# Expert products in plain float32 on four column groups, with a ring of 14 weight blocks

## The chip, the cores and the metric

The kernel runs on one core of a Trainium2 chip. The metric is the device time of one launch in microseconds (us). TensorE multiplies, reading from the on-chip memory and writing into eight banks of accumulators; VectorE, ScalarE and GpSimd work elementwise; SyncE here only issues transfers. The engines run on their own and meet at semaphores.

## The reference

One inference step of a trunk of two layers for 256 prompt tokens and 8 x 4 sample tokens (288 in all, width 1024), in float32. Layer 0 has gated linear attention and a dense SwiGLU, layer 1 an mLSTM and a mixture of 8 experts, two for each token. The change touches the mixture alone:

```
probs = softmax(x @ w_router + b_router)
top_p, top_i = top_k(probs, 2);  top_p = top_p / sum(top_p)
gates = sum(one_hot(top_i, 8) * top_p[..., None], axis=-2)
for e in range(8):
    g, u = split(x @ w_gu[e], 2)          # w_gu[e]: 1024 x 7168
    y = y + gates[:, e:e+1] * ((silu(g) * u) @ w_down[e])   # w_down[e]: 3584 x 1024
```

An expert's weights are 44.0 MB of float32, all eight 352 MB, read once.

## The kernel before

Everything ahead of the mixture (both mixers, the dense block, router, table of tokens) runs first. Then comes a loop over items, one item for an expert with up to 96 of its tokens (`CAP`); with these inputs it makes 8 passes. In one pass:

- **Weights.** The 44 MB come as 42 blocks (`PER`) of 1 MB into a ring of 7 (`RING`), each 128 partitions x 2048 floats (`SLOT`). A gate or up block has four row tiles of 512 columns (rows of 2 KB in memory), a down block two row tiles of 1024 columns (rows of 4 KB). SyncE issues a load when `wlo_ready` says that VectorE has finished with the block seven back (line 739).
- **Split.** TensorE multiplies here in the faster format float32r, which keeps fewer bits. So every block is split: `weight_hi` on ScalarE (line 2142) writes the rounded part into `w_hi`, `weight_lo` on VectorE (line 2874) the rest into `w_lo`, each with three places (`SPLIT`). The tokens (`xg_hi`, `xg_lo`) and the activations (`aT_hi`, `aT_lo`) are split as well, and `three` (lines 1090 to 1092) makes each product of hi x hi, hi x lo and lo x hi, with 96 stationary columns of tokens and 512 moving columns of weights. Some of these tiles lie in memory called `hT_split` or `hT`; the profile shows those names.
- **Steps.** The 3584 hidden columns are taken in 7 steps (`STEPS`) of 512. `project("g", n)` and `project("u", n)` fill gate and up banks, two of each (`GB`, `UB`) in turn. ScalarE takes Silu of the gate bank (line 2182), VectorE multiplies with the up bank (line 2934), `turn_act` transposes the result on TensorE (line 1724) one step later, and `down` adds its product into the banks `YB`, behind the up product of the next step.
- **End of a pass.** `next_tokens` transposes the next expert's tokens (line 1753). `item_rows` (line 1673) turns the next item's gates and rows. In the next pass ScalarE scales the finished output into `ye` (`read_output`), GpSimd adds it into rows in memory (a scatter with addition) and gathers the tokens for the pass after.

The last item's output stays on the chip: `read_output` and `output_lo` split it, and `scatter` (lines 1688 and 1689) spreads it over the tokens with matmuls, before the final norm.

Each engine runs its instructions in the order in which they are written. `loop_full(b, k, i)` waits until bank b is filled for the k-th time in pass i, `loop_before(b, k, i)` until it is free for that.

Of the kernel before, what the change touches and what calls it, by code (L numbers as in the profile page):

```python
# [24 lines left out]
P = 128  # L25
# [7 lines left out]
TT = 3  # L33
# [16 lines left out]
RING = 7  # L50
EARLY_RING = 4
LATE_ORDER = (6, 4, 5, 2, 3, 0, 1)
SPLIT = 3
# [9 lines left out]
WIDE = 512  # L63
STEPS = FE // WIDE
HALF = KT // 2
PER = 6 * STEPS
# [140 lines left out]
GB, UB, YB, TB, MB = (0, 1), (2, 3), (4, 5), 6, 7  # L207
LAST = ((GB[0], 0), (GB[1], 0), (UB[0], 0), (UB[1], 0), (TB, 0), (MB, 1))
GAB = (GB[1], UB[1])
GATE_ROW = 32  # L210
LOW_ROW = 32
LOOP_TURNS = {0: 4, 1: 4, 2: 4, 3: 4, 4: 1, 5: 1, 6: STEPS, 7: 1}
# [4 lines left out]
def trunk_kernel(nc, ins, outs):  # L217
# [5 lines left out]
    with ExitStack() as ctx:  # L223
# [6 lines left out]

        with nc.sbuf_tensor("ring", [P, RING * SLOT], F32) as ring:
            pass
        ring_lo = sb("ring_lo", [P, RING * SLOT], F32R)
# [43 lines left out]
        rank_rows = sb("rank_rows", [RANK, 10, T])  # L277
# [123 lines left out]
        w_hi = es("w_hi", [P, SPLIT, SLOT], F32R)  # L401
        w_lo = es("w_lo", [P, SPLIT, SLOT], F32R)
        xg_hi = es("xg_hi", [P, KT, CAP], F32R)
        xg_lo = es("xg_lo", [P, KT, CAP], F32R)
        aT_hi = [es("aT_hi", [P, 4, CAP], F32R)[:, :, :]]
        aT_lo = [es("aT_lo", [P, 4, CAP], F32R)[:, :, :]]
        for n, a in enumerate((aT_hi, aT_lo)):
            at = 3 * WIDE + n * 4 * CAP
            a.append(hT_split[:, at:at + 4 * CAP].rearrange("p (f c) -> p f c", f=4))
        h_tok = es("h_tok", [P, TT, D])  # L410
        x_acc = es("x_acc", [P, TT, D])
        hT_flat = hT[0:CAP, :, :].rearrange("p k t -> p (k t)")
        sg = hT_flat[:, 0:2 * WIDE].rearrange("p (a n) -> p a n", a=2)
        act = hT_flat[:, 2 * WIDE:3 * WIDE]
# [31 lines left out]
        whi_ready = sem("whi_ready")  # L446
        wlo_ready = sem("wlo_ready")
        hi_ready = sem("hi_ready")
        split_used = sem("split_used")
# [114 lines left out]
        def expert_slot(j):  # L564

            s = LATE_ORDER[j % RING]
            return ring[:, s * SLOT:(s + 1) * SLOT], s
# [48 lines left out]
        late_free = [full("L1r5"), full("L1r7"), full("L1r7"), full("L1w1"), full("L1w3"), full("L1w5"), full("L1w7")]  # L616
# [33 lines left out]
        expert_order = [(k, 0, x) for k in "gu" for x in range(2)]  # L650
        for j in range(1, STEPS):
            expert_order += [(k, j - (k == "d"), x) for k in "gud" for x in range(2)]
        expert_order += [("d", STEPS - 1, x) for x in range(2)]
        assert len(expert_order) == PER
        expert_at = {x: n for n, x in enumerate(expert_order)}

# [4 lines left out]
        def split_free(eng, j, i):  # L661

            if j == SPLIT - 1:
                eng.wait_ge(bank_full[YB[1]], i + static_turns[YB[1]])
                return
            if j < SPLIT:
                used_ = i * SPLIT_COUNT + (split_counts[PER - SPLIT + j] - SPLIT_COUNT + 2)
            else:
                kind, nth, x = expert_order[j - SPLIT]
                if kind != "d" and x == 1:  # L670
                    eng.wait_ge(*loop_full((GB if kind == "g" else UB)[nth % 2], nth // 2, i))
                    return
                used_ = i * SPLIT_COUNT + (split_counts[j - SPLIT] + 2)
            eng.wait_ge(split_used, used_)


        token_after = {2: (0,), 3: (1, 2), 4: (3,), 5: (4,), 6: (5,), 7: (6, 7)}

        split_counts, SPLIT_COUNT = {}, 0
        for j, (kind, nth, x) in enumerate(expert_order):  # L680
            if (kind != "d" and x == 0) or (kind == "d" and j < PER - 1):
                SPLIT_COUNT += 1
                split_counts[j] = SPLIT_COUNT
        HI_TURNS = STEPS + 2

        def turned_hi(ac, nth, i):

            ac.wait_ge(*loop_full(TB, nth, i))
            ac.activation(aT_hi[nth % 2], psum[TB][:, 0:4 * CAP].rearrange("p (f c) -> p f c", f=4), ACT.Copy).then_inc(hi_ready, 1)
# [5 lines left out]
        def _(sp):  # L695
# [33 lines left out]
            def load(e, j):  # L729
                kind, nth, x = expert_order[j]  # L730
                dst, s = expert_slot(j)
                if kind == "d":
                    r = nth * WIDE + x * 2 * P
                    src = w_dn[bass.ds(e, 1), r:r + 2 * P, :].rearrange("e (t p) n -> p (e t) n", p=P)
                else:
                    c = nth * WIDE + (FE if kind == "u" else 0)
                    src = w_gu[bass.ds(e, 1), x * HALF * P:(x + 1) * HALF * P, c:c + WIDE].rearrange("e (t p) n -> p (e t) n", p=P)
                out = dst.rearrange("p (k n) -> p k n", k=src.shape[1])
                sp.dma_start(out, src).then_inc(slot_loaded[s], 16)

            for j in range(PER):
                if j < RING:
                    sp.wait_ge(*late_free[j])
                else:
                    sp.wait_ge(wlo_ready, j - RING + 1)
                load(0, j)
# [287 lines left out]
        def _(pe):  # L1034
# [664 lines left out]
            with pe.Fori(0, n_items) as i:  # L1699
# [27 lines left out]
                def down(nth, xs=(0, 1)):  # L1727
                    pe.wait_ge(*loop_before(TB, nth + 1, i))
                    if nth == 0:
                        output_read(i)  # L1730
# [1278 lines left out]
```

## Time and profile before

| | |
|---|---|
| median of 3 runs | 1524.95 us (1524.89 to 1526.27) |
| profiled execution, its span | 1524.6 us |
| TensorE busy | 1508.8 us, 99% |
| VectorE, ScalarE, GpSimd busy | 1219.2, 1009.9, 186.9 us |
| moved by transfers | 449.97 MB, mean 295 GB/s |
| matmul records | 8481 |

The loop over experts takes the span from 547.9 us to about 1510; some 14 us follow. The times of matmuls in the profile overlap, since they are pipelined: what a matmul costs is read from how far apart two starts are. A plain float32 matmul has two records, a float32r matmul one. In a form such as 128\*96, 128x512 the first pair is the stationary operand (rows by columns), the second the moving one. The rows below are not repeated here.

### The profile page before, as it was taken

To read this page: it belongs to the slowest core of one execution; us is meant where nothing else is said; L and a number is where in the kernel's file an instruction comes from. 1 tells how busy PE (TensorE), PEld (TensorE's weight loads), DVE (VectorE), ACT (ScalarE), POOL (GpSimd) and SP (SyncE) were. 2 spreads that over 40 slices of the span, in tenths; PEclk is the share of its full clock that TensorE was granted. 3 is DMA by queue.
4 is the path that set the end of the run, shared out by engine and by line. 5 is a ranking of instruction groups with operands and counts; after the bars stand their busy time and mean duration, and the time that the engine had idled before them with its cause. 6 is when DMAs were issued, how large, how long until landed. Compare 5 with 4: busy or idle time off the path is not lost.

```text
span 1524.6 us, 22920 instructions
## 1 busy us (share of the span) xinstructions
PE 1508.8 (99%) x8481; PEld 1196.9 (79%) x8481; DVE 1219.2 (80%) x1189; ACT 1009.9 (66%) x871; POOL 186.9 (12%) x224
## 2 busy tenths in 40 slices
PE   9999999999999999999999999999999999999997
PEld 7999999999998977777776776776776777767775
DVE  6758766646776688888889888888888888888888
ACT  5646533335546487787787777778778778778776
POOL 3334100002234150000000000000000000000010
PEclk9999999999999999999999999999999999999999
DMA  7467555455453689999999999999999999999993
GB/s 215 140 198 234 163 166 166 159 180 181 141 136 112 219 298 388 383 350 394 375 348 394 371 364 380 370 366 376 377 379 361 376 382 358 377 383 355 387 372 131
DMA packets 234264, 449.97 MB, mean 295 GB/s; under 512 B 16713, under 2 KB 83345, under 8 KB 234209
## 3 DMA queue, kind: packets, MB, share of 16 engines
q1 hardware_dynamic: 226208, 422.98, 77.5%
q0 software_dynamic: 7376, 24.53, 5.6%
q10 hardware_dynamic: 624, 1.70, 0.3%
q8 instruction: 37, 0.61, 0.2%
q14 instruction: 19, 0.15, 0.0%
HBM read 434.62 MB, written 14.57 MB: 295 GB/s over the span
## 4 chain that ended last, share of the span: by engine, by line
PE 96%; DVE 2%; ACT 1%; issue 1%; DMA 0%; SPq 0%; DVEq 0%; ACTq 0%
PE bank L1090 29%; PE bank L1092 29%; PE bank L1091 29%; PE bank L1724 1%; PE bank L1328 1%; PE bank L1058 0%; PE bank L1317 0%; PE bank L1658 0%; PE bank L1638 0%; PE bank L1296 0%; PE bank L1753 0%; DMA par_rows<-in_mlstm_g_norm_dram 0%; PE bank L1554 0%; PE bank L1308 0%; PE bank L1239 0%
## 5 line engine op out<-in xcount | busy, mean ns | idle before, releaser
L2874 DVE TENSOR_TENSOR w_lo<-ring,w_hi 128x2048 fp32r<-128x2048 f32 x337 | 771.4, 2291 | 121.6 <-ACT w_hi L2142 120.1
L2142 ACT ACTIVATE w_hi<-ring 128x2048 fp32r<-128x2048 f32 x337 | 645.4, 1918 | 223.5 <-PE bank L1092 223.4
L1090 PE MATMUL bank<-w_hi,xg_hi 128*96 128x512 f32 x896 | 355.9, 397 | 1.0 <-DVE xg_lo L2884 1.0
L1092 PE MATMUL bank<-w_hi,xg_lo 128*96 128x512 f32 x896 | 353.4, 394 | 0.0
L1091 PE MATMUL bank<-w_lo,xg_hi 128*96 128x512 f32 x896 | 351.8, 393 | 0.0
L1092 PE MATMUL bank<-work_split,ring_lo 128*128 128x288 f32 x920 | 271.4, 295 | 0.0
L1090 PE MATMUL bank<-work_split 128*128 128x288 f32 x904 | 268.8, 297 | 0.5 <-DVE ring_lo L2319 0.4
L1091 PE MATMUL bank<-work_split 128*128 128x288 f32 x904 | 266.0, 294 | 0.0
L1092 PEld LDWEIGHTS bank<-w_hi,xg_lo 128*96 128x96 f32 x896 | 144.6, 161 | 63.1
L1090 PEld LDWEIGHTS bank<-w_hi,xg_hi 128*96 128x96 f32 x896 | 144.5, 161 | 61.3 <-DVE w_lo L2874 2.1
L1091 PEld LDWEIGHTS bank<-w_lo,xg_hi 128*96 128x96 f32 x896 | 144.9, 162 | 59.7
L1092 PEld LDWEIGHTS bank<-work_split,ring_lo 128*128 128x128 f32 x920 | 172.8, 188 | 0.0
L1090 PEld LDWEIGHTS bank<-work_split 128*128 128x128 f32 x904 | 169.9, 188 | 3.5 <-issue 1.6
L1091 PEld LDWEIGHTS bank<-work_split 128*128 128x128 f32 x904 | 170.0, 188 | 0.2
L1847 ACT ACTIVATE work_split<-ring 128x2048 fp32r<-128x2048 f32 (+1 forms) x49 | 91.8, 1875 | 85.8 <-PE bank L1092 76.7
L2506 DVE TENSOR_TENSOR ring_lo<-ring,work_split 128x2048 fp32r<-128x2048 f32 (+1 forms) x34 | 75.6, 2224 | 34.3 <-ACT work_split L1847 34.2
L1092 PE MATMUL bank<-w_hi,aT_lo 128*96 128x512 f32 x256 | 101.1, 395 | 0.0
L1090 PE MATMUL bank<-w_hi,aT_hi 128*96 128x512 f32 x256 | 100.7, 393 | 0.0
L1091 PE MATMUL bank<-w_lo,aT_hi 128*96 128x512 f32 x256 | 100.4, 392 | 0.0
L1024 POOL TENSOR_TENSOR turn_mark<-pad_row 1x1 f32<-1x1 f32 x8 | 17.8, 2231 | 509.6 <-DVE row_next L2897 509.6
L1090 PE MATMUL bank<-w_hi,hT_split 128*96 128x512 f32 x192 | 76.6, 399 | 0.0
L1091 PE MATMUL bank<-w_lo,hT_split 128*96 128x512 f32 x192 | 75.8, 395 | 0.0
(456 smaller groups left out, 1686.4 us busy)
## 6 DMA issues: line engine op xcount, KB each, us to landing
ring<-in_moe_w_gu_dram SPq DMA_DIRECT2D x225, 1024.0 KB, 6.3
ring<-in_moe_w_down_dram SPq DMA_DIRECT2D x112, 1024.0 KB, 6.2
ring<-in_ffn_w_gu_dram SPq DMA_DIRECT2D x22, 1024.0 KB, 5.1
ring<-in_gla_w_in_dram SPq DMA_DIRECT2D x12, 1024.0 KB, 5.4
ring<-in_mlstm_w_in_dram SPq DMA_DIRECT2D x12, 1024.0 KB, 5.3
ring<-in_ffn_w_down_dram SPq DMA_DIRECT2D x8, 1024.0 KB, 5.0
out_dram<-work POOLq DMA_DIRECT2D x9, 512.0 KB, 4.5
work<-in_state_gla_S_dram POOLq DMA_DIRECT2D x8, 512.0 KB, 7.5
```

The source lines that it names most:

```text
L1024: gp.tensor_tensor(turn_mark[:, :], pad_row[0:1, :], pad_row[0:1, :], ALU.add).then_inc(marked, 1)
L1090: pe.matmul(out, w_hi_, x_hi, start=first, stop=False, skip_group_check=True)
L1091: pe.matmul(out, w_hi_, x_lo, start=False, stop=False, skip_group_check=True)
L1092: return pe.matmul(out, w_lo_, x_hi, start=False, stop=last, skip_group_check=True)
L1328: mm = pe.matmul(bk[:, m * n:(m + 1) * n], v_tok[0:n, tt, g * P:(g + 1) * P], scores(g), start=(m == 0), stop=done, skip_group_check=True)
L1724: mm = pe.transpose(psum[TB][:, f * CAP:(f + 1) * CAP], act[:, f * P:(f + 1) * P], ident[0:CAP, 0:CAP])
L1847: ac.activation(hi, raw, ACT.Copy).then_inc(fhi_ready, 1)
L2142: ac.activation(w_hi[:, j % SPLIT, :], src, ACT.Copy).then_inc(whi_ready, 1)
L2506: ve.tensor_tensor(lo, raw, hi.bitcast(F32), ALU.subtract).then_inc(flo_ready, 1)
L2874: ve.tensor_tensor(w_lo[:, j % SPLIT, :], src, w_hi[:, j % SPLIT, :].bitcast(F32), ALU.subtract)\
```

## The change

The expert products are made in plain float32, without `w_hi`, `w_lo`, `weight_hi`, `weight_lo` and the split of tokens and activations. The 96 tokens are three tiles of 32 (`TILE`, `TILES`). A matmul now has 32 stationary columns, 256 moving columns, and one of four column groups of the array: its output goes to 32 of the 128 partitions of a bank. Three token tiles and four groups don't fit each other, so the fourth group takes another part of the product: in a step's first two column halves (`gate, 0` and `gate, 1`), bank AB holds three tiles of half 0 and one of half 1, BB the same of up, CB the four that are left. For the output, columns 768 to 1023 are spread over the fourth groups of the other three quarters.

```
-RING = 7
+RING_MEM = 7
-LATE_ORDER = (6, 4, 5, 2, 3, 0, 1)
+LATE_ORDER = (6, 4, 5, 2, 7, 3, 0, 12, 13, 1, 8, 9, 10, 11)
+RING = len(LATE_ORDER)
+WIDTHS = (512,) * 7
-GB, UB, YB, TB, MB = (0, 1), (2, 3), (4, 5), 6, 7
+AB, BB, CB, YB, TB, MB = 0, 1, 2, (4, 5), (6, 3), 7
...
+                def gate_up(s, xs):
+                    n = WIDTHS[s] // 2
+                    per = SLOT // (4 * n)
+                    for x in xs:
+                        w = weights("gu", s, x)
+                        for k in range(per):
+                            kt = x * per + k
+                            gate, up = (w[:, (4 * k + o) * n:(4 * k + o + 2) * n].rearrange("p (c n) -> p c n", c=2) for o in (0, 2))
+                            x_tile = [xg[:, kt, a * TILE:(a + 1) * TILE] for a in range(TILES)]
+                            for b, units in ((AB, ((gate, 0, 0), (gate, 0, 1), (gate, 0, 2), (gate, 1, 0))),
+                                             (BB, ((up, 0, 0), (up, 0, 1), (up, 0, 2), (up, 1, 0))),
+                                             (CB, ((up, 1, 1), (up, 1, 2), (gate, 1, 1), (gate, 1, 2)))):
+                                if first:
+                                    pe.wait_ge(*loop_before(b, s, i))
+                                for group, (m, c, a) in enumerate(units):
+                                    mm = part(psum[b][:, 0:n], group, x_tile[a], m[:, c, :], first, last)
+                                    if b == AB and group == 0 and k == 0:
+                                        mm.then_inc(slot_begun, 1)
...
+                            for d, b in enumerate((YB[0], YB[0], YB[1])):
+                                for group, (m, a) in enumerate(((d, 0), (d, 1), (d, 2), (3, d))):
+                                    mm = part(out, group, act_tile(s, x, t, a), w[:, t, m, :], first and d != 1, last)
...
+                gate_up(0, range(2 * blocks(0)))
+                for s in range(1, STEPS):
+                    gate_up(s, range(2))
+                    turn_act(s - 1)
...
+                    gate_up(s, range(2, 2 * blocks(s)))
+                    if s < STEPS - 1:
+                        down(s - 1, range(blocks(s - 1)))
+                s = STEPS - 1
+                down(s - 1, range(2))
+                next_tokens(i)
+                turn_act(s)
+                down(s - 1, range(2, blocks(s - 1)))
+                down(s, range(blocks(s)))
```

- **Banks.** Gate, up and the mixed bank exist once each (before, two of gate and two of up). The transposed activations take two banks (`TB`), one copied by VectorE (128x256), one by ScalarE (128x128). A step has four transposes, two of 128 and two of 64 moving columns.
- **ScalarE and VectorE** per step: Silu of AB (128x256) and of half of CB (64x256), and the two multiplications `act1` and `act2`.
- **Ring.** 14 blocks instead of 7, the new seven in the memory of `w_hi` and `w_lo`. A load may start once TensorE has begun the block after the one that lay there (`slot_begun`), without the other engines. A gate/up block holds two row tiles of 512 gate and 512 up columns, loaded by two transfers of 512 KB; a down block has two neighbouring rows for each partition, rows of 8 KB:

```
-                    src = w_dn[bass.ds(e, 1), r:r + 2 * P, :].rearrange("e (t p) n -> p (e t) n", p=P)
+                    src = w_dn[bass.ds(e, 1), r:r + 2 * P, :].rearrange("e (p t) n -> p (e t) n", t=2)
```

- **Output.** `last_quarter` on VectorE gathers columns 768 to 1023 from the fourth groups (three copies, then a scaling), ahead of the steps of each pass and once behind the loop, where it stands ahead of `output_lo`.

```
+            last_quarter(n_items)
             output_lo(0)
             ve.wait_ge(*loop_full(MB, 0, n_items))
...
             output_lo(1)
+            output_lo(2)
```

ScalarE, head of a pass, before: Silu of the first gate bank (bank 0), with the table load ahead of it; between them stand copies of blocks into `w_hi`.

```order
L2156 ACTIVATE xT<-bank,slot_gate 96x512 [waits bank_free5,bank_full5]
L2139 REGISTER_ALU
L674 REGISTER_ALU [waits slot_loaded2]
L2142 ACTIVATE w_hi<-ring 128x2048 [waits split_used]
L671 ISA [waits slot_loaded3]
L2142 ACTIVATE w_hi<-ring 128x2048 [waits bank_full0]
L2181 REGISTER_ALU [waits bank_full0]
L2182 ACT_TABLE_LOAD
L2182 ACTIVATE hT<-bank,one_col 96x512 [waits bank_free2]
```

And now, with bank 0 for AB, bank 1 for BB and bank 2 for CB:

```order
L2167 ACTIVATE xT<-bank,slot_gate 96x256 [waits bank_free5,bank_full5]
L2184 ISA
L2185 REGISTER_ALU [waits bank_full0]
L2186 ACT_TABLE_LOAD
L2186 ACTIVATE hT<-bank,one_col 128x256 [waits bank_free1]
L2187 ISA
L2188 REGISTER_ALU [waits bank_full2]
L2189 ACTIVATE hT<-bank,one_col 64x256 [waits bank_free2]
```

The copies are gone; the table load still stands behind the wait for bank 0 and ahead of Silu.

TensorE, end of a pass, before: the last transposes of activations (line 1724) stand between two halves of the down product of step 5 (12 matmuls each).

```order
L1092 MATMUL bank<-w_hi,hT_split 96x512
L1724 MATMUL bank<-ident,hT 128x96 [waits bank_free6,bank_free2]
L1724 MATMUL bank<-ident,hT 128x96 x3
L1703 REGISTER_ALU [waits bank_free6]
L1090 MATMUL bank<-w_hi,hT_split 96x512 [waits wlo_ready]
L1091 MATMUL bank<-w_lo,hT_split 96x512
```

And now (banks 6 and 3 hold the transposed activations; `rank_rows` is the memory of tokens and activations):

```order
L1693 MATMUL bank<-ring,rank_rows 32x256 x23
L1769 ISA
L1772 REGISTER_ALU [waits gathered]
L1775 MATMUL bank<-ident,xT 128x96 [waits bank_free0]
L1775 MATMUL bank<-ident,xT 128x96 x3
L1775 MATMUL bank<-ident,xT 128x96 [waits bank_free1]
L1775 MATMUL bank<-ident,xT 128x96 x3
L1728 MATMUL bank<-ident,hT 128x128 [waits bank_free6,bank_free3,bank_free2,bank_free1]
L1728 MATMUL bank<-ident,hT 128x128
L1733 MATMUL bank<-ident,hT 128x64 x2
L1750 REGISTER_ALU [waits bank_free6,bank_free3]
L1688 REGISTER_ALU [waits bank_free3]
```

The whole down product of step 5 stands ahead of the transposes, and that of step 6, which reads what they make, right behind them.

## Rows read from the trace of the kernel before

**Rows 1.** The page: busy time by engine, and the chain that ended last.

```profile
PE 1508.8 (99%) x8481; PEld 1196.9 (79%) x8481; DVE 1219.2 (80%) x1189; ACT 1009.9 (66%) x871; POOL 186.9 (12%) x224
PE 96%; DVE 2%; ACT 1%; issue 1%; DMA 0%; SPq 0%; DVEq 0%; ACTq 0%
```

**Rows 2.** The loop: length, busy us by engine, clock, share and GB/s of transfers.

```profile
668.00:1500.00 832.00, 832.00 (x3777) 585.08 (x3776) 725.54 (x456) 631.65 (x428) 43.44 (x32) 1.00 1.02 372
```

**Rows 3.** TensorE in one pass by form: count, busy us and mean ns, idle.

```profile
L1091 PE MATMUL bank<-w_lo,xg_hi 128*96 128x512 f32 x112 | 44.0, 393 | 0.0
```

**Rows 4.** Timeline of TensorE around `next_tokens`, two passes: start, us, instruction.

```profile
655.66 0.39 PE L1091 MATMUL bank<-w_lo,xg_hi 128*96 128x512 f32 x1
655.89 0.39 PE L1092 MATMUL bank<-w_hi,xg_lo 128*96 128x512 f32 x1
656.12 0.82 PE L1753 MATMUL bank<-ident,xT 96*128 96x96 f32 x8
...
776.42 0.82 PE L1753 MATMUL bank<-ident,xT 96*128 96x96 f32 x8
```

**Rows 5.** Line 1368 and its neighbours: durations (min/median/max ns), timeline, one stretch as above.

```profile
L1368 PE MATMUL bank<-work x64: 379/379/403, 103.7 to 107.0; 128*32 128x256 f32 x64
...
102.80 0.94 PE L1328 MATMUL bank<-work 32*128 32x32 f32 x7
103.67 3.66 PE L1368 MATMUL bank<-work 128*32 128x256 f32 x64
107.26 0.98 PE L1308 MATMUL bank<-work_split 128*128 128x256 f32 x6
...
104.00:104.40 0.40, 0.40 (x16) 0.23 (x12) 1.00 1.04 420
```

**Rows 6.** Timeline of TensorE at its densest stretch.

```profile
465.63 1.97 PE L1328 MATMUL bank<-work 32*128 32x32 f32 x16
467.52 0.63 PE L1554 MATMUL bank<-work,head_col 32*8 32x32 f32 x16
468.08 0.63 PE L1589 MATMUL bank<-work,head_col 128*8 128x32 f32 x16
...
468.86 3.71 PE L1604 MATMUL bank<-work 128*64 128x128 f32 x64
```

**Rows 7.** ScalarE and VectorE by form; the last two are of the whole kernel.

```profile
L2182 ACT ACT_TABLE_LOAD x1 | 1.3, 1283 | 0.0
...
L2874 DVE TENSOR_TENSOR w_lo<-ring,w_hi 128x2048 fp32r<-128x2048 f32 x43 | 98.4, 2290 | 15.7 <-ACT w_hi L2142 15.5
...
L2922 DVE TENSOR_TENSOR aT_lo<-bank,aT_hi 128x384 fp32r<-128x384 f32 x4 | 2.2, 552 | 0.0
...
L1898 ACT ACTIVATE work<-bank 128x256 f32<-128x256 f32 x16 | 5.2, 379 | 19.3 <-PE bank L1152 19.3
...
L2296 DVE TENSOR_TENSOR work<-bank,rbc 128x256 f32<-128x256 f32 x16 | 6.7, 420 | 9.1 <-PE bank L1092 9.0
```

**Rows 8.** Waits of SyncE's queue from 560 to 1500: us in total, times, longest.

```profile
SPq L739 <- DVE w_lo L2874: 734.5, 325, 3.6
```

**Rows 9.** Transfers: first pass's q8, queues of 668 to 1500 (first, last), a small one, 580 to 600.

```profile
q8 instruction: 5, 0.08, 0.3%
...
q1 hardware_dynamic: 127236, 302.51, 98.5%
...
q14 instruction: 3, 0.02, 0.0%
...
out_dram<-par_rows POOLq DMA_DIRECT2D x1, 16.0 KB, 2.0
...
580.00:600.00 20.00, 20.00 (x97) 14.21 (x96) 17.22 (x10) 14.55 (x10) 0.00 (x0) 1.00 1.05 393
```

**Rows 10.** Timeline behind the loop: `ye_lo` on VectorE, the first scattering matmul.

```profile
1509.97 0.75 DVE L2234 SCALAR_TENSOR_TENSOR ye_lo<-bank,slot_gate,ye_hi 96x512 fp32r<-96x512 f32 x1
...
1511.65 0.49 PE L1688 MATMUL bank<-ye_hi,selT 96*128 96x512 f32 x1 [0.72 <-DVE selT L2961]
```

More of the change, by code:

```diff
@@ L62 @@
 N_STATIC = 2 * N_MIX + N_FFN
-WIDE = 512
-STEPS = FE // WIDE
+WIDTHS = (512,) * 7
+STEPS = len(WIDTHS)
+STARTS = [sum(WIDTHS[:s]) for s in range(STEPS)]
 HALF = KT // 2
-PER = 6 * STEPS
+TILE = 32
+TILES = CAP // TILE
+QUARTERS = D // 4
 WORK = 24576
@@ L648, in out_parts, with blocks @@
             return raw, out_hi[l][n], ring_lo[:, s * SLOT:(s + 1) * SLOT]
[L650 to L654, printed above, removed]
-        expert_at = {x: n for n, x in enumerate(expert_order)}
+        def blocks(s):
+            return WIDTHS[s] // (2 * P)
@@ new lines, in part @@
+                def part(out, group, stationary, moving, first, last):
+                    return pe.matmul(out[group * TILE:(group + 1) * TILE, :], stationary, moving, start=first, stop=last, skip_group_check=True)
+                def gate_up(s, xs):
[3 more added lines that the diff above has]
+                        w = weights("gu", s, x)
+                        for k in range(per):
+                            kt = x * per + k
+                            gate, up = (w[:, (4 * k + o) * n:(4 * k + o + 2) * n].rearrange("p (c n) -> p c n", c=2) for o in (0, 2))
+                            x_tile = [xg[:, kt, a * TILE:(a + 1) * TILE] for a in range(TILES)]
+                            first, last = kt == 0, kt == KT - 1
+                            for b, units in ((AB, ((gate, 0, 0), (gate, 0, 1), (gate, 0, 2), (gate, 1, 0))),
[7 more added lines that the diff above has]
+                                        mm.then_inc(slot_begun, 1)
+                                if last:
+                                    mm.then_inc(bank_full[b], 1)
@@ new lines, in act_tile, with down @@
+                def act_tile(s, x, t, a):
+                    n = WIDTHS[s] // 2
+                    c, y = divmod(x, n // (2 * P))
+                    q = 2 * y + t
+                    if c == 0 or a == 0:
+                        at = q * P + (a if c == 0 else TILES) * TILE
+                        return aT[s % 2][0][:, at:at + TILE]
+                    at = q * 64 + (a - 1) * TILE
+                    return aT[s % 2][1][:, at:at + TILE]
+                def down(s, xs):
+                    for b in TB:
+                        pe.wait_ge(*loop_before(b, s + 1, i))
+                    if s == 0 and xs[0] == 0:
@@ L2962, in _ @@
             output_lo(1)
+            output_lo(2)
             ve.wait_ge(x_back, 48)
```

353 lines of the change are left out of this document (157 added, 196 removed).

## The prediction

> **What bounds the kernel now.** I read the page first: TensorE is busy 99% of the span and the chain that ended last is 96% TensorE [rows 1]. Then the stretches: in the 832 us from 668 to 1500, all of it the loop over experts, TensorE is never idle and its clock is fully granted (1.00, the 2.4 GHz level), VectorE and ScalarE are busy 87% and 76%, and the transfers run at 372 GB/s with a share of 1.02 [rows 2]. So the loop is bound by TensorE, with the transfers close behind. How long is one expert? The eight transposes of the next tokens come once per expert, at 656.12 and at 776.42 [rows 4]: 120.3 us, eight times, 962.4 us of the span.
>
> What is in these 120.3 us? 42 blocks of 12 matmuls, 504 in all (28 blocks of gate and up give 336, of which 112 for each of three lines, [rows 3]), and the spacing of neighbours is 0.23 us (655.66, 655.89, 656.12 in [rows 4]; their 0.39 us of duration overlap). 504 x 0.232 = 117 us; 28 transposes, 8 of next tokens at 0.082 us ((0.82 - 0.25)/7) and 6 records of `item_rows` are the other 3.4 us. A split matmul of 512 columns is thus spaced by 0.232 us, though 512 columns at 2.4 GHz are 0.213.
>
> **The change, part by part.**
>
> *The products.* Float32 shows as two records per matmul, each of two cycles per column. The kernel before has this very shape once: line 1368 multiplies with 32 stationary columns, 256 moving columns, four column groups, 32 matmuls, 64 records [rows 5]. They start at 103.67 and the next line at 107.26, 3.59 us for 16 rounds of four records; without the two changes of tiling (below) 16 x 0.216 = 3.46. So four matmuls run at once and a round of four costs 2 x 0.216 = 0.432 us, and this while transfers ran at 420 GB/s (the stretch from 104.0 in [rows 5]). The changed loop needs per step 8 row tiles x 3 rounds for gate and up and 4 x 3 for down: 36 rounds, 252 per expert. 252 x 0.432 = **108.9 us**, against 117. The array does as many column cycles as before; the gain is the spacing of 216 against 232 ns.
>
> *Transposes.* Per step two with 128 moving columns (0.11 us, as line 1328 in [rows 5]: (0.94 - 0.27)/6) and two with 64, between nothing and 0.11; I take 0.07, a little under the 0.082 of 96 columns. 14 x 0.11 + 14 x 0.07 + 8 x 0.082 + 0.5 = **3.7 us**.
>
> *Changes of tiling.* Into line 1368: previous start plus 0.112 would be 103.58, it is 103.67: 0.09. Out: 0.13 (above). 0.22 us for there and back, six times per expert (the seventh lies in a stall, below): **1.3 us**. Bounds: nothing, and double.
>
> *New wait 1.* Gate, up and their mixed bank are now single (AB, BB, CB), and after step 0 no down product stands between two gate/up groups. ScalarE's order in the changed kernel has a table load behind the wait on bank 0: the load of 1.28 us [rows 7] starts only when AB is full. AB is full some 0.2 us after its last round, then 1.28 + about 0.45 for Silu on 256 columns (the 0.38 of a copy [rows 7] plus its bias), then 0.2 to TensorE: 2.25 us, of which rounds of BB and CB cover 0.86. **1.4 us** per expert. Behind it queue VectorE's two multiplications (0.42 each [rows 7]), which arrive just in time for BB and CB. In later steps the down product (5.2 us) covers the same chain.
>
> *New wait 2.* At the end of an expert, `turn_act(6)` is followed at once by `down(6)`, where before half a down product (2.8 us) stood between. VectorE first copies half of the new tokens (128x384, 0.55 [rows 7]), then the transposed activations (about 0.42): some 1.25 us after the transposes began, plus 0.2, against 0.35 of work: **1.1 us**.
>
> *Code.* The loop's body grows from 543 matmuls to 1047. In the first pass five pieces of code were fetched, in the next 832 us q8, the queue that carries code, has no line (q1 first, q14 last), so the body stayed at hand [rows 9]. Whether a body of twice the size does, no row shows. If not, each return to the loop's head waits for a fetch. A piece has 16 KB, and the nearest transfer of 16 KB took 2.0 us from issue to landing [rows 9]. Bounds: nothing, and 4 us for a loaded queue; I take 1.2 us for each of 7 returns, since matmuls already queued cover a part: **8 us**. The Trainium skill ("Runtime: NRT & Kernel Launch", Instruction fetch mechanics) gives TensorE room for 2048 instructions, refilled in blocks, and says that a taken branch to code outside the window stalls; by it this body (two instructions per matmul, 2094) would just not fit. The trace agrees only as far as that the smaller body fitted.
>
> *What goes.* 42 copies of whole blocks on ScalarE and 42 subtractions of 2.29 us on VectorE per expert [rows 7]. Both lay beside TensorE, so they give back nothing; they only stop being next in line.
>
> *Transfers.* 44.0 MB of weights per expert as before plus 0.8 of rows. The ring of 14 blocks lets some 12 be loaded before 548 us. SyncE waited for free blocks 734.5 us of the loop [rows 8], so 372 GB/s was what was asked for; from 580 to 600 it was 393 [rows 9]. Down rows of 8 KB instead of 4 should cost no more. 346 MB must land in 940 us: 368 GB/s. **Nothing**, as long as that is given.
>
> *Ends.* Behind the loop VectorE now moves the last quarter (three copies and a scaling, some 0.4 us each) before `output_lo(0)`, which scattering waits for; before, `ye_lo` began at 1509.97 and scattering at 1511.65 [rows 10]. With the third `output_lo`: **+2 us**. Ahead of the loop one subtraction goes: -0.4.
>
> *Sum.* 108.9 + 3.7 + 1.3 + 1.4 + 1.1 = 116.4 us; x 8 = 931.2; + 8.4 of code = 939.6, against 962.4. 1524.6 - 962.4 + 939.6 + 1.6 = 1503.4. The median of the runs is 0.35 above the span, so **1504 us**.
>
> **Rivals.**
>
> *TensorE's dispatch is the bound (slower).* The loop asks for a record pair (weights and matmul) every 54 ns for 110 us on end; before it was every 232. Line 1368 asked it only for 3.5 us, out of a filled queue. For: the densest stretch has 16 + 16 + 64 records (and one of a transpose) from 467.52 to 472.57 [rows 6], 52 ns each, and is no longer than 5 us. Against: it held without a gap, and records 29 ns apart just before it ((0.63 - 0.19) / 15, lines 1554 and 1589) left little queued for the 64. It decides above 54 ns. If the rate were that of the stretch from 465.63, 113 records in 6.9 us or 61 ns, an expert took 2016 x 0.061 + 7.5 = 130.5 us, the kernel 1524.6 + 8 x 10.2 + 10 = some 1615. The Trainium skill ("TensorE: Matmul & The Clock Gate", Back-to-back issue gap) has about 62 ns per matmul of sequencer time as a possible bound; by it the time would be the same, some 1620. The 52 ns of this trace speak against it.
>
> *Transfers are the bound.* 12 or 13 blocks in flight may give less than two did. At 360 GB/s the 346 MB take 961 us, the last lands at 1509, and with 3 us for its products and 16 behind the loop the kernel takes 1528; it is slower than before under 361, and binds at all under 368. For: the share of 1.02 says that the engines always had a packet. Against: 393 above, and SyncE's waits.
>
> *All covers hold.* No code fetch, no cost of retiling, half the stalls: 114 us per expert, 1476.
>
> *The groups don't run at once.* Then an expert would take over 400 us. Line 1368 excludes it.
>
> **How the numbers follow.** TensorE bound with the terms above, 1485 to 1520: 0.62. All covers hold, 1474 to 1485: 0.08. Transfers bound: 0.12, half of it under 1522, the rest 1522 to 1535. Fetches or stalls larger than taken, up to 1540: 0.06. Dispatch bound, 1560 to 1650: 0.10. Groups not at once, or an order I misread: 0.02. The range from 1478 to 1532 leaves out dispatch, the last case and the edges. A measurement tells about 0.2%, 3 us, from no change: faster 0.80, same 0.06, slower 0.14.
>
> **What would show it.** Right: rounds of four records every 216 ns; an expert every 116 to 118 us; gaps of TensorE at two places only, behind step 0 (ended by ScalarE, with a table load in it) and before the last down product (ended by VectorE); q8 lines in the loop if code is fetched again. Wrong: gaps put down to issue all over the rounds, spaced over 54 ns per record (dispatch); TensorE waiting for blocks of the ring (transfers); rounds longer than 0.432 us without any gap (then the row of line 1368 did not carry over to a long stretch). In either of the last two the sum fails in its first term.

## The result, and the profile after

The changed kernel takes 1582.9 us (median of 4 runs, 1579.6 to 1584.5) against 1525.6 us of the kernel before (4 runs beside it): ratio 1.037, interval 1.036 to 1.039. It is slower by 3.7%, where 1.4% faster was forecast, and the time lies 51 us above the range. The profiled execution has a span of 1582.7 us.

The page of the changed kernel: busy time, chain, products and the queue that carries code. The first and the third line answer to [rows 1].

```profile
PE 1507.8 (95%) x20577; PEld 1085.0 (69%) x20577; DVE 474.1 (30%) x935; ACT 377.9 (24%) x583; POOL 153.2 (10%) x224
...
q8 instruction: 182, 2.98, 0.8%
...
PE 90%; issue 4%; DVE 4%; ACT 1%; DMA 0%; SPq 0%; DVEq 0%; ACTq 0%
...
L1693 PE MATMUL bank<-ring,rank_rows 128*32 128x256 f32 x16128 | 908.2, 385 | 59.0 <-issue 44.8
```

VectorE and ScalarE are relieved as meant (80% and 66% to 30% and 24%), TensorE is still the chain, but it is busy 95% in place of 99%, and 4% of the chain is "issue": time in which nothing that the profile shows was waited for. The loop in windows (columns as in [rows 2]): all of it, a stretch without a return to the loop's head, and one with.

```profile
668.00:1500.00 832.00, 777.58 (x13262) 454.36 (x13266) 77.00 (x222) 80.86 (x166) 21.10 (x32) 0.96 0.96 349
...
1200.00:1300.00 100.00, 100.00 (x1762) 59.77 (x1755) 9.42 (x28) 7.57 (x19) 1.12 (x2) 1.00 1.01 376
1300.00:1400.00 100.00, 89.90 (x1537) 52.46 (x1539) 9.47 (x28) 10.21 (x20) 2.75 (x4) 0.95 0.94 338
```

Where nothing returns, TensorE is full, at full clock, and executes 1762 records in 100 us. Where the loop returns, 10 us are idle and the clock is lower. The timeline of TensorE there (start, us, instruction, count, in brackets the idle time before and what ended it), and the windows of the same place:

```profile
664.24 2.13 PE L1693 MATMUL bank<-ring,rank_rows 128*32 128x256 f32 x36
670.79 0.83 PE L1693 MATMUL bank<-ring,rank_rows 128*32 128x256 f32 x9 [4.43 <-issue]
674.14 8.13 PE L1693 MATMUL bank<-ring,rank_rows 128*32 128x256 f32 x108 [2.51 <-issue]
...
664.50:672.50 8.00, 2.70 (x45) 1.17 (x37) 1.63 (x4) 1.04 (x2) 1.65 (x2) 0.94 0.82 252
...
672.50:682.00 9.50, 7.86 (x108) 4.07 (x112) 0.00 (x0) 0.00 (x0) 0.00 (x0) 0.69 0.66 199
```

Two stalls, 4.43 and 2.51 us, with nine records between them, and then a clock of 0.69: most of the stretch from 672.5 to 682 ran at the 1.2 GHz level (in windows of 2 us the clock is 1.00 until 670, then 0.90, then 0.50 from 672 to 678, 0.89, and 1.00 from 680). The expert's products themselves are not slow. The waits of TensorE from 560 to 1560 (total, times, longest) show the same twice per return, 14 times in seven returns:

```profile
PE bank L1693 <- issue: 44.8, 14, 4.8
...
PE bank L1693 <- ACT hT L2186: 7.6, 7, 1.1
PE bank L1693 <- ACT rank_rows L2174: 4.3, 7, 0.6
```

So the two stalls of a return are 6.4 us on average (44.8 / 7), the first 4.09 to 4.80, the second 1.18 to 3.60. The trace also holds a record of the branch itself, which the page leaves out. It lasts 5.2 to 5.9 us at each of the seven returns; in the kernel before it lasts 0.21 to 0.24.

And one trip of the loop, 1050.1 to 1178.7, in the transfers (packets, MB, share) and in the window:

```profile
q8 instruction: 19, 0.31, 1.0%
...
1050.10:1178.70 128.60, 121.05 (x2066) 70.64 (x2062) 11.98 (x34) 12.65 (x26) 2.76 (x4) 0.96 0.96 351
```

The body is fetched anew on every trip, 19 packets of 16 KB, where the kernel before had no line of q8 in its loop [rows 9]. A pass takes 128.5 us ((1558.3 - 787.3) / 6, from starts of `next_tokens`), against 120.3 before [rows 4] and 117.6 by my sum. The same window also corrects a count: 2066 matmul and 2062 weight load records lie in the window of a pass (some cross its edges; 2058 of each start in it), each an instruction. A float32 matmul is two pairs of weight load and matmul, not one; the body has 4,187 instructions, not the 2,094 of the prediction (all records of TensorE and its sequencer in a trip; before, 1,168).

### The profile page after: what moved, and what is told of

It reads as the page before. It is cut to its first block, busy times and chain, and to the rows that moved or that the text cites. A ratio compares the mean times of both kernels' runs of the same rounds, so it can differ in the third digit from the quotient of the medians.

```text
span 1582.7 us, 46658 instructions
## 1 busy us (share of the span) xinstructions
PE 1507.8 (95%) x20577; PEld 1085.0 (69%) x20577; DVE 474.1 (30%) x935; ACT 377.9 (24%) x583; POOL 153.2 (10%) x224
## 4 chain that ended last, share of the span: by engine, by line
PE 90%; issue 4%; DVE 4%; ACT 1%; DMA 0%; SPq 0%; DVEq 0%; ACTq 0%
PE bank L1693 57%; PE bank L1073 8%; PE bank L1075 8%; PE bank L1074 8%; PE bank L1728 1%; PE bank L1733 1%; PE bank L1309 1%; DVE ring_lo L2284 1%; PE bank L1775 0%; PE bank L1041 0%; PE bank L1298 0%; PE bank L1639 0%; PE bank L1619 0%; PE bank L1277 0%; DMA par_rows<-in_mlstm_g_norm_dram 0%
## 5 line engine op out<-in xcount | busy, mean ns | idle before, releaser
L1693 PE MATMUL bank<-ring,rank_rows 128*32 128x256 f32 x16128 | 908.2, 385 | 59.0 <-issue 44.8
L1693 PEld LDWEIGHTS bank<-ring,rank_rows 128*32 128x32 f32 x16128 | 519.2, 111 | 424.5 <-issue 77.8
L2935 DVE COPY rank_rows<-bank 128x256 f32<-128x256 f32 x56 | 23.7, 423 | 426.2 <-PE bank L1728 426.2
L2953 DVE TENSOR_TENSOR hT<-hT,bank 128x256 f32<-128x256 f32 x56 | 23.6, 421 | 378.6 <-ACT hT L2186 378.6
L2186 ACT ACTIVATE hT<-bank,one_col 128x256 f32<-128x256 f32 x56 | 26.5, 474 | 207.5 <-PE bank L1693 207.4
L1002 POOL TENSOR_TENSOR turn_mark<-pad_row 1x1 f32<-1x1 f32 x8 | 1.5, 183 | 702.3 <-DVE xT L2928 702.3
L1074 PE MATMUL bank<-hT_split,ring_lo 128*128 128x288 f32 x128 | 37.8, 295 | 0.0
L2284 DVE TENSOR_TENSOR ring_lo<-ring,work_split 128x2048 fp32r<-128x2048 f32 x15 | 34.6, 2307 | 7.6 <-ACT work_split L1867 7.5
L1073 PE MATMUL bank<-ring_lo 128*128 128x288 f32 x112 | 34.2, 305 | 0.1
L1075 PE MATMUL bank<-ring_lo 128*128 128x288 f32 x112 | 33.0, 295 | 0.0
L1728 PEld LDWEIGHTS bank<-ident,hT 128*128 128x128 f32 x112 | 17.5, 205 | 19.8 <-issue 19.8
```

The lines of the kernel that those rows point to most:

```text
L1073: pe.matmul(out, w_hi_, x_hi, start=first, stop=False, skip_group_check=True)
L1074: pe.matmul(out, w_hi_, x_lo, start=False, stop=False, skip_group_check=True)
L1075: return pe.matmul(out, w_lo_, x_hi, start=False, stop=last, skip_group_check=True)
L1693: return pe.matmul(out[group * TILE:(group + 1) * TILE, :], stationary, moving, start=first, stop=last, skip_group_check=True)
L1728: mm = pe.transpose(psum[TB[0]][:, q * P:(q + 1) * P], act1[:, 2 * P * y + t:2 * P * (y + 1):2], ident[:, :])
L2186: ac.activation(sg1[:, 0:n], psum[AB][:, 0:n], ACT.Silu, bias=zero).then_inc(bank_free[AB], 1)
```

## The experiments

All times are medians. The kernel before, run beside each group, took 1526.1 us (e1 to e4), 1525.0 (e5 to e8) and 1526.3 (e9 to e12), so a difference between runs of two groups is uncertain by about 1 us.

**e1: no return.** TensorE's pass is written out seven times, and its loop runs once.

```
-            with pe.Fori(0, n_items) as i:
+            def one_pass(i):
...
+            for n in range(7):
+                one_pass(n)
+            with pe.Fori(7, n_items) as i:
+                one_pass(i)
```

> The changed kernel with TensorE's expert pass written out seven times ahead of its loop, which then runs once: the same matmuls, waits and transfers, but no backward branch on TensorE's path. Theory (the missed time is instruction fetch at the seven returns of a loop of about 4,100 instructions): each pass loses the gaps of 4.8 and 2.9 us after the branch and the stretch at 1.2 GHz behind them, about 11 us in all, so 1583 - 7 x 11 = about 1505 us, granted clock 1.00 in every window of the expert stage, pass about 117.5 us. Rival A (matmuls are bound by dispatch, or the four column groups interfere): the pitch inside the passes does not change and the time stays within 5 us of 1583. Rival B (transfers take over once TensorE is not held up): the pass cannot be shorter than 44.04 MB at the rate of the undisturbed window 1200:1300 (376 GB/s), 117.1 us, so the same 1505 but with waits on the ring in the list of waits; if the rate sustained over all passes is only 349 GB/s, the pass is 126 us and the time about 1570.

Measured: 1515.9 us (ratio 0.9937, 0.992 to 0.9953), 67.0 us less than the changed kernel, 9.6 for each of seven returns. The loop's window and page lines of e1:

```profile
668.00:1450.00 782.00, 770.43 (x13550) 474.06 (x13546) 78.02 (x224) 82.20 (x169) 20.92 (x31) 1.00 1.03 380
...
L1693 PE MATMUL bank<-ring,rank_rows 128*32 128x256 f32 x16128 | 884.7, 379 | 14.3 <-ACT hT L2190 9.3
```

The clock is 1.00 throughout, "issue" is gone from the idle time, the transfers give 380 GB/s with SyncE waiting on TensorE for 434 of these 782 us, not the other way round. Dispatch is no bound: a record pair goes out every 54 ns on average, pass after pass. So the returns cost more than the kernel lost (67 us of 57), and the changed products are worth having. But the pass is 118.8 us ((1489.7 - 776.9) / 6), not 117.5, and the time 11 us above the theory's 1505. That rest is in other terms of the sum (e7, and the next section).

**e2: a hint ahead of the branch.**

```
-            with pe.Fori(0, n_items) as i:
+            with nc.Fori(0, n_items, engines=..., hint_back_edge=True) as i:
```

> The changed kernel, with one instruction more at the head of TensorE's loop: a hint that names the branch back, so that its target can be fetched ahead. Theory (code fetch at the returns): the hint takes away the first of the two gaps (4.8 us), perhaps the second (2.9 us) and with them the fall of the clock: 1583 - 7 x 5 = 1548 if only the first goes, 1505 if both go. Rival (the gap is not a fetch but the loop's register work, or some engine that is waited for): within 5 us of 1583.

Measured: 1566.4 us, 2.4 us less per return. Both stalls are still there; one return in the timeline of TensorE:

```profile
911.44 5.39 PE L1693 MATMUL bank<-ring,rank_rows 128*32 128x256 f32 x96 [0.61 <-ACT rank_rows L2174]
919.71 0.68 PE L1693 MATMUL bank<-ring,rank_rows 128*32 128x256 f32 x8 [2.88 <-issue]
922.59 1.93 PE L1693 MATMUL bank<-ring,rank_rows 128*32 128x256 f32 x16 [2.20 <-issue]
```

The hint names only code, and it moves the stall: this is about fetching. But it takes neither gap away, and my 1548 was too hopeful: together they go from 6.4 to 4.5 us on average (31.3 us in seven returns). The branch record falls from 5.2 to 5.9 us to 2.4 to 3.8. The last packet of q8 ahead of the branch's end starts 0.0 to 1.4 us behind the branch's start, without the hint 2.7 to 3.5, so that block is asked for earlier. The packet behind it still starts only after the branch's end, in every return of both kernels.

**e3: the kernel before with a body of two passes.** Nothing of the change is in this kernel.

```
-            with pe.Fori(0, n_items) as i:
-                (one pass)
+            with pe.Fori(0, n_items, 2) as i:
+                one_pass(i)
+                one_pass(i + 1)
```

> The kernel before, with two expert passes in each trip of TensorE's loop (four trips, three returns; some 2,280 instructions in the body where there were 1,140). Arithmetic, waits and transfers are those of before. Theory (a body that does not stay loaded is fetched again at each return and the chip stalls there): 3 returns x about 8 to 11 us = 1550 to 1559 us; the instruction queue shows some ten packets per return in the second half of the span, where before had none. Rival (the stalls of the changed kernel come from its column groups, its ring or its other order, not from the size of the loop): 1525.6 within 3 us.

Measured: 1542.7 us (1.0113, 1.0096 to 1.013), 5.5 us for each of three returns. One trip of it (q8, window), and its return in the timeline:

```profile
q8 instruction: 11, 0.18, 0.3%
...
1029.60:1275.50 245.90, 242.44 (x1094) 169.90 (x1093) 209.94 (x133) 183.09 (x125) 11.37 (x8) 0.99 1.01 366
...
1033.62 0.47 PE L1090 MATMUL bank<-w_hi,xg_hi 128*96 128x512 f32 x1 [0.51 <-issue]
...
1038.89 0.74 PE L1090 MATMUL bank<-w_hi,xg_hi 128*96 128x512 f32 x1 [2.96 <-issue]
1039.42 0.63 PE L1091 MATMUL bank<-w_lo,xg_hi 128*96 128x512 f32 x1
1039.85 0.63 PE L1092 MATMUL bank<-w_hi,xg_lo 128*96 128x512 f32 x1
```

(The window counts records, 1094 + 1093; with registers and branch a trip has 2,334 instructions.) The mechanism needs neither column groups nor the larger ring: a kernel whose loop was free of it gets it when its body doubles. The price was missed: 5.5 us, not 8 to 11. The second gap is not far from that in the changed kernel (2.96 and 2.51), the first is 0.51 in place of 4.43. Two things differ. The matmuls still queued at the branch are spaced by 0.23 us here and by 0.054 there, so here they cover more: they run 3.5 us past the start of the branch. And the branch record itself is shorter, 3.5 to 3.9 us for 5.2 to 5.9; why, the runs don't show. Behind the gap matmuls of 512 columns start 0.43 us apart (1039.42 and 1039.85), the 1.2 GHz level; ahead of it, 0.23.

**e4: wider steps, the loop kept.**

```
-WIDTHS = (512,) * 7
+WIDTHS = (1024, 1024, 1024, 512)
```

> The changed kernel with gate and up in steps of 1024, 1024, 1024 and 512 columns in place of seven of 512: 512-column matmuls for three quarters of the expert's input products, and 1,440 matmul records in a pass in place of 2,016, some 2,950 instructions; rows of 4 KB for the wide steps. Theory (code): the body is still too long to stay loaded, so the seven stalls stay: about 1583, less 0 to 8 us for the steps that are no longer there. Rival (each instruction costs dispatch time, or the price of a return goes with the length of the body): 720 fewer instruction pairs x 8 passes x some ns each, or stalls a third shorter: 1555 or less.

Measured: 1563.1 us (1553.6 to 1564.3), 20 less than the changed kernel, and outside both expectations. With e7, the same steps without a return, it comes apart: e4 - e7 is 72.6 us, 10.4 per return, no less than for the longer body (9.6). So the price does not go with the length of a body that is too long. The 20 us are not code: without any return the same steps save 25 (e7).

**e5: the table of Silu early.** On top of e1.

```
                 for b, ins_ in read_output(i, ye):
                     ins_.then_inc(bank_free[b], 1)
+                ac.activation(silu_seed[:, 0:1], one, ACT.Silu, bias=zero)
```

> The unrolled kernel (e1), with one Silu of a single column per partition put behind ScalarE's read of the outputs at the head of its pass, so that the table of Silu is loaded (1.28 us) before the first gate columns are complete, and not behind the wait for them. Theory (the stall of 1.55 us between step 0 and step 1 of every pass is this table load): the gap shrinks to some 0.3 us, 8 x 1.25 = 10 us less: about 1506 us. Rival (the stall is the Silu itself with the release of the bank, or the copies of VectorE): the gap stays above 1.2 us and the time at 1515 to 1516.

Measured: 1507.0 us, 8.9 less than e1. ScalarE in e1 (first two lines) and in e5 (last three):

```profile
794.01 1.28 ACT L2190 ACT_TABLE_LOAD   x1 [8.94 <-PE bank L1693]
795.30 0.47 ACT L2190 ACTIVATE hT<-bank,one_col 128x256 f32<-128x256 f32 x1
```

```profile
782.35 1.28 ACT L2184 ACT_TABLE_LOAD   x1
783.64 0.30 ACT L2184 ACTIVATE spare<-one_col 128x1 f32<-128x1 f32 x1
791.37 0.47 ACT L2191 ACTIVATE hT<-bank,one_col 128x256 f32<-128x256 f32 x1 [7.44 <-PE bank L1693]
```

The load now lies in idle time, and the stall behind step 0 (1.55 us between two starts) is 0.41. Wait 1 of the prediction was right in place, cause and size.

**e6: a down product behind the last turn.** On top of e1.

```
-                down(s - 1, range(2))
+                down(s - 1, range(1))
                 next_tokens(i)
                 turn_act(s)
-                down(s - 1, range(2, blocks(s - 1)))
+                down(s - 1, range(1, blocks(s - 1)))
```

> The unrolled kernel (e1), with the last block of down(5) moved behind the last turn of the activations, as the kernel before had it; 5.2 us of matmuls then stand between the turn of step 6 and down(6). Theory (the gap of 0.84 us at that place is the wait for the copies of the turned activations): it shrinks to the 0.21 us of the other such places, 8 x 0.63 = 5 us less: about 1511 us. Rival (another wait takes its place: the gather of the next tokens or the activations of step 6 are now asked for 2.6 us earlier): the same time, or up to 8 x 2 us more.

Measured: 1510.6 us, 5.3 less. TensorE at this place in e1 and in e6:

```profile
777.64 0.43 PE L1728 MATMUL bank<-ident,hT 128*128 128x128 f32 x2
778.00 0.45 PE L1733 MATMUL bank<-ident,hT 64*128 64x64 f32 x2
779.01 15.75 PE L1693 MATMUL bank<-ring,rank_rows 128*32 128x256 f32 x288 [0.56 <-ACT rank_rows L2178]
```

```profile
775.28 0.45 PE L1733 MATMUL bank<-ident,hT 64*128 64x64 f32 x2
775.66 5.60 PE L1693 MATMUL bank<-ring,rank_rows 128*32 128x256 f32 x100
```

Wait 2 is real, 0.66 us in a pass where I took 1.1.

**e7: wider steps without a return.** e1 with the edit of e4.

> The unrolled kernel (e1) with the steps of 1024, 1024, 1024 and 512 columns: four turns of the activations in a pass in place of seven. Theory (between two matmuls of the experts a turn takes about 1.1 us of TensorE, 0.9 more than the matmul round it follows, and that was undersized in my sum): three turns less in each of 8 passes, 2.8 us, make the pass 116.0 and the time about 1494. Rival (the transfers are at their limit: the windows of e1 show a share of 1.02 to 1.03 and 375 to 385 GB/s): 44.04 MB in 116.0 us are 380 GB/s; at 375 the pass is 117.4 and the time 1505, with waits on the ring.

Measured: 1490.5 us (0.9766, 0.9749 to 0.9782), 25.4 less than e1. The pass is 115.7 us ((1463.7 - 769.7) / 6), 3.1 less. The last turn of a pass and a wide one:

```profile
770.43 0.43 PE L1728 MATMUL bank<-ident,hT 128*128 128x128 f32 x2
...
771.16 31.17 PE L1693 MATMUL bank<-ring,rank_rows 128*32 128x256 f32 x384
...
808.19 0.74 PE L1728 MATMUL bank<-ident,hT 128*128 128x128 f32 x4
...
809.48 0.67 PE L1654 MATMUL bank<-gate_token,sel 128*96 128x2 f32 x6
```

The transposes are as many as before, 28 in a pass, but in four turns in place of seven. From its first transpose to the instruction behind it a wide turn takes 1.29 us (808.19 to 809.48), two narrow ones take 2 x 0.81 (e1), and the change of tiling ahead of it comes once in place of twice: some 1.5 of the 3.1 us. Wait 2 is gone as well (770.43 to 771.16 is 0.73, for 1.37 in e1), which is 0.6, and the stall behind step 0 is 0.6 shorter (0.57 of idle time for 1.17). The other 0.4 us lie in the 144 rounds of 512 columns: one starts every 0.429 us, for 2 x 0.216. So what wider steps give here is not the turns alone. The transfers follow:

```profile
668.00:1450.00 782.00, 778.13 (x9922) 344.58 (x9918) 69.84 (x166) 69.74 (x111) 21.12 (x32) 1.00 1.01 388
```

388 GB/s, where 375 was my rival's limit.

**e8 to e10: how long a body stays.** The kernel before, two passes per trip, with products left out to shorten the code. The helpers `two` and `one` are `three` without its last, and without its last two, matmuls.

```
-                            mm = three(psum[b][0:CAP, :], ...
+                            mm = (two if kind == "g" else three)(psum[b][0:CAP, :], ...
...
-                                mm = three(psum[YB[half]][0:CAP, :], ...
+                                mm = two(psum[YB[half]][0:CAP, :], ...
```

> The kernel before with two passes in each trip as in e3, but without the third of the three split products (the one with the low part of the activations) in the gate columns and in down: that part of the arithmetic is left out, and two passes have about 1,830 instructions in place of 2,280. Only the returns are looked at. Theory (what fits in the instruction memory is not fetched again, and the limit lies between the two): no fetches of the instruction queue after the first trip, and no gap over 0.5 us at the three returns; the Trainium skill (Runtime: NRT & Kernel Launch, Instruction fetch mechanics) puts TensorE's limit at 2,048. Rival (any body longer than that of before, 1,140, is fetched again): about seven packets per trip and gaps of 1 and 3 us at each return, as in e3.

> As e8, with the third of the three products left out everywhere: two passes of the kernel before in a trip, about 1,660 instructions (six and a half blocks of 256, where one packet of the instruction queue is one block). e8 was fetched again with 1,890 instructions, so a plain limit of 2,048 is out. Theory now (the fetcher runs on in sequence two blocks past the branch at the end of the loop, e8 took ten packets a trip for a body of eight, and these two push out the head): the body and two more blocks have to fit in eight; seven or eight blocks and two are nine or ten, so it is fetched again, about nine packets a trip, with the gaps of 5 and 3 us. Rival (the limit lies just under e8's size): no packets after the first trip.

> As e9, with the second product of the gate columns left out too: about 1,440 instructions in a trip, which lie in six or seven blocks of 256. Theory (body and two blocks ahead have to fit in eight): where the body touches six blocks nothing is fetched after the first trip and the returns cost nothing; where it touches seven it is fetched again. Rival (anything that is longer than the 1,170 instructions of before is fetched again): about eight packets a trip and gaps of 5 and 3 us at each return.

A trip of e8, then of e9 (q8 and window of each), and the windows of a trip of e10, in whose transfers q8 has no line, with its return:

```profile
q8 instruction: 9, 0.15, 0.3%
...
1001.40:1232.50 231.10, 204.46 (x869) 131.56 (x870) 207.47 (x133) 181.22 (x125) 11.88 (x8) 0.98 1.04 387
```

```profile
q8 instruction: 9, 0.15, 0.3%
...
1000.50:1231.30 230.80, 183.88 (x757) 112.25 (x757) 207.07 (x133) 180.54 (x125) 11.89 (x8) 0.98 1.04 388
```

```profile
1000.90:1230.80 229.90, 173.17 (x645) 105.90 (x645) 208.31 (x133) 181.10 (x125) 11.88 (x8) 0.89 1.04 390
...
1002.42 0.39 PE L1095 MATMUL bank<-w_hi,aT_lo 128*96 128x512 f32 x1
1002.91 1.18 PE L1090 MATMUL bank<-w_hi,xg_hi 128*96 128x512 f32 x4
```

With what is neither matmul nor weight load, the trips have 1,886, 1,662 and 1,438 instructions. The first two are fetched again, the third is not, and the stalls go with the fetch: e9 has six gaps put down to "issue", 20.4 us in all, e10 has none. The branch records say the same: 6.2 to 7.6 us in e8, 6.2 to 6.3 in e9, 0.22 to 0.25 in e10. My expectation for e8 was wrong: the Trainium skill ("Runtime: NRT & Kernel Launch", Instruction fetch mechanics) gives TensorE room for 2,048 instructions, and here 1,662 already do not stay; the measurement decides. The corrected theory was stated before e9 and e10, and both agree with it (e10 if its body touches six blocks and not seven): the fetcher runs one or two blocks past the end of the body, and what it brings in pushes out the head. A packet is a block of some 256 instructions (e1 takes 97 packets for six passes of 4,187, 259 each), and the trips of e3, e8, e9 and the changed kernel took 11, 9 to 10, 9 and 19 packets for bodies of 10, 8, 7 and 17 blocks. A plain limit somewhere between 1,438 and 1,662 fits as well; the two are not told apart. The return of e8 (TensorE, timeline):

```profile
1001.29 0.47 PE L1090 MATMUL bank<-w_hi,aT_hi 128*96 128x512 f32 x1 [0.96 <-DVE w_lo L2882]
...
1002.98 0.40 PE L1091 MATMUL bank<-w_hi,aT_lo 128*96 128x512 f32 x1
1008.03 0.74 PE L1090 MATMUL bank<-w_hi,xg_hi 128*96 128x512 f32 x1 [4.66 <-issue]
...
1013.56 0.59 PE L1090 MATMUL bank<-w_hi,xg_hi 128*96 128x512 f32 x1 [1.80 <-issue]
```

Here TensorE had waited for VectorE just before (the low parts of the weights), so that only eight matmuls, 2.1 us, were left when the branch began at 1001.40. The branch lasted 6.2 us, and the first gap is 4.66 us. The times of these three (1488.0, 1486.7 and 1483.4, one run each) say nothing of the returns: VectorE is at 90% and the transfers are at 387 to 390 GB/s with a share of 1.04, so that a part of each stall may have been covered by time that TensorE would have waited anyway.

**e11: the best version.** e7 with the edit of e5.

> e7 (unrolled, steps of 1024, 1024, 1024 and 512 columns) with the one-column Silu of e5. Theory: the gap of 1.16 us between step 0 and step 1 goes down to some 0.4 us, 8 x 0.75 = 6 us less: about 1484 to 1485. Rival (the transfers, 44.04 MB in a pass of 114.9 us or 383 GB/s, take over): the gain stays under 2 us and waits on the ring show.

Measured: 1485.5 us (0.9731, 0.9714 to 0.9747), 5.0 less than e7 and 40.7 less than the kernel before.

```profile
668.00:1450.00 782.00, 782.00 (x9998) 346.95 (x9994) 71.06 (x167) 70.60 (x117) 19.75 (x31) 1.00 1.00 387
```

TensorE has no idle time left, its pass is 115.1 us, and SyncE still waits for it for 540 us of these 782 (359.3 and 180.9, its two lines), so the transfers don't bind.

**e12: the kernel before without a return.** The edit of e1 in the kernel before.

> The kernel before with TensorE's pass written out seven times ahead of its loop, as e1 did it with the changed one. Theory (a body of 1,170 instructions stays loaded, so its returns cost nothing): 1525 within 2 us, though the instruction queue then shows some five packets in every pass. Rival (each return of any loop, or the code that is read in sequence, has a price of its own): 5 us or more off 1525 in either direction.

Measured: 1525.9 us against 1526.3, ratio 0.9997 (0.9988 to 1.0007), with four packets of q8 in 120 us of the loop. A return of a body that stays costs nothing, and code that is read in sequence costs nothing; the 67 us of e1 are not a gain from unrolling as such.

## Why the prediction was wrong, point by point

- **Code: wrong, and this decided it.** The step took 1.2 us for each of seven returns, with bounds of nothing and 4 us; e1 gives 9.6. Three things failed in it. The count: 2,094 instructions for 4,187, though the page of before counts matmul and weight load records apart and x64 records for 32 matmuls stood in [rows 5]. The price: I took one transfer of 16 KB (2.0 us, [rows 9]) and let the queued matmuls hide part. There are two in series, with 4.3 and 2.1 us of idle time on average: the packet of the second starts only after the branch has ended (5.9 to 8.9 us behind the branch's start, which lasts 5.2 to 5.9), and a queue of matmuls 54 ns apart covers little. The consequence: the clock falls during the idle time (to 0.50 from 672 to 678), and the matmuls behind it run at the 1.2 GHz level. 9.6 less 6.4 us of gaps leaves 3.2. The 183 records behind the second gap take 12.2 us on average and would take 10.1 at the spacing of e1, and the nine between the gaps take 1.48 us in six of seven returns for 0.83 in the first: together some 2.7 of the 3.2 us. Both my bounds held only one fetch.
- **Products: right.** 252 rounds of 0.432 us. In e1 the 72 rounds from 779.01 last 15.75 us; 72 x 0.216 is 15.55, and the last is as long as a record. The row of line 1368 carried over from 3.5 us to eight passes.
- **Transposes and changes of tiling: undersized.** I took 0.58 us for a turn (0.36 of transposes, 0.22 of changes) from short transposes of another kind. A turn in e1, on TensorE:

```profile
802.77 15.75 PE L1693 MATMUL bank<-ring,rank_rows 128*32 128x256 f32 x288
818.45 0.51 PE L1728 MATMUL bank<-ident,hT 128*128 128x128 f32 x2
818.89 0.45 PE L1733 MATMUL bank<-ident,hT 64*128 64x64 f32 x2
819.26 7.11 PE L1693 MATMUL bank<-ring,rank_rows 128*32 128x256 f32 x127
```

  288 records are 72 rounds of four (a round here is one record of each group), and the next would start at 802.77 + 72 x 0.216 = 818.32; it starts at 819.26. A turn is 0.94 us, six of them 2.2 us more than taken (the seventh stands with wait 2). `next_tokens` and `item_rows` are undersized in the same way: with the changes around them they take 0.85 and 0.73 us for 0.66 and 0.5, another 0.4.
- **Wait 1: right.** 1.55 us between two starts in place of 0.2, so 1.35 for 1.4, with the table load in it, removed in the main by moving that load (e5: 1.1 per pass). The prediction's own terms, 0.2 + 1.28 + 0.45 + 0.2, add up to 2.13 and not 2.25; with that it would have been 1.3.
- **Wait 2: right in place, too large.** Taken 1.1; 5.3 us in eight passes are 0.66 (e6). The wait and the last turn together are 1.37 us (777.64 to 779.01), for 1.1 + 0.36. The page puts the end of the wait down to ScalarE's copy and not to VectorE's, which I had named, but VectorE's ended only 0.03 us earlier (778.73 and 778.76). What I had too small is the work beside it: 0.74 us in e6, for 0.35.
- **The sum of a pass without code:** 116.4 + 2.2 + 0.4 - 0.05 - 0.1 = 118.85, measured 118.8. Of the missed 79 us (1582.9 - 1504), 67 are the returns, of which 8 were in the sum, and 8 x 2.4 = 19 are the turns and their like, less what the two waits were taken too large. 59 + 19 = 78.
- **Transfers, ends, relief of VectorE and ScalarE: right.** 376 GB/s where TensorE did not stall, no wait for the ring; outside the passes e1 takes 1513.9 - 8 x 118.8 = 563.5 us, by my sum 563.8.
- **Rivals.** Dispatch is out (e1, 54 ns in every pass; the sum would have been some 1615). Its range, 1560 to 1650, does hold the measured 1583, but by chance: its mechanism is not there. (Its time for 62 ns per matmul is a slip: 2016 x 0.062 + 7.5 is 132.5 us, and by the same sum the kernel would take some 1632 us, not 1620.) The transfers are out (388 GB/s in e7). "Fetches or stalls larger than taken" had 0.06 and ended at 1540; it was the case, beyond its end. The rule of the Trainium skill ("Runtime: NRT & Kernel Launch", Instruction fetch mechanics) that I cited, a taken branch to code outside the window stalls, agrees with the branch records of these runs, and I gave it a price without a row that shows one. An unknown cost that repeats per pass should have widened the range instead.

## What to carry to other kernels

Count the instructions of a hardware loop's body, and count a float32 matmul as four (two pairs of weight load and matmul); look for the instruction queue in windows of the loop, where it should have no line. If a change takes the body over about 1,400 instructions on TensorE, unroll, or shorten the body: here a return then cost 5.5 to 10.4 us. Matmuls still queued at the branch cover a part of it. An edit that gives each matmul less to do, or more instructions, makes the body longer: here 504 float32r matmuls of two instructions became 1,008 float32 ones of four, and the body went from 1,168 to 4,187.

## What the runs showed of the hardware that I had not expected

- A return to a body that did not stay costs two stalls in series (4.43 and 2.51 us in one return of the changed kernel, 4.66 and 1.80 in e8, 0.51 and 2.96 in e3, where more of the branch was covered), and then a stretch at the 1.2 GHz level. The branch record lasts 3.5 to 7.6 us there, and 0.2 us where the body stays.
- A turn of two transposes of 128x128 and two of 64x64 between products on column groups costs 0.94 us (e1).
- The whole body is fetched again, not its excess: 1,662 instructions take 9 packets a trip, 1,438 take none. Straight code of the same kind is fetched without any stall (e1, e12).
- A branch hint saved 2.4 of 9.6 us (e2).
- The transfers give 387 to 390 GB/s over a long stretch (388 in e7, 387 in e11, 390 in e10), more than the 372 at which the kernel before ran.
